# A merge's gate products issued between the steps of two attentions, with score tiles sharing PSUM banks

## What is computed

```python
h = rms_norm(x, g_norm1[l]) * (1.0 + sc1) + sh1
u = h @ w_in[l] + b_in[l]
q_lat, kv_lat, k_rope, q_sb, k_sb, v_sb, gate_mla, gate_sb = jnp.split(u, IN_SPLIT_POINTS, axis=-1)
...
y_mla = causal_softmax_attention(q, k, v_mla)           # 4 heads, 192 per head for q and k, 128 for v
y_sb = stick_breaking_attention(q_sb, k_sb, v_sb)       # 4 heads of 128
# stick breaking: l = log_sigmoid(-z) before the diagonal; a = exp(z + reverse_cumsum_keys(l)); y = a @ v
merged = (jax.nn.sigmoid(gate_mla) * (y_mla @ w_branch_mla[l])
          + jax.nn.sigmoid(gate_sb) * (y_sb @ w_branch_sb[l]))
x = x + gt1 * (merged @ w_out[l])
```

## Time and profile before

| what | value |
|---|---|
| median of 3 runs | 3700.75 us (3700.08, 3700.75, 3716.53) |
| span of the profiled execution | 3710.6 us |
| PE busy | 3287.6 us (89%) |
| DVE, ACT, POOL busy | 1128.7, 652.6, 189.4 us |
| chain that ended last | PE 83%, DMA 6%, DVE 5%, issue 4%, ACT 3% |

### The profile page before, as it was taken

The page is one execution under the profiler, slowest core; times in us unless marked ns, Lnnn a source line. Parts: engine busy times, 40 slices in busy tenths (PEclk is TensorE's granted clock), DMA queues, the critical chain, the costliest instruction groups (busy, mean ns, idle before and its releaser), DMA issues.

```text
span 3710.6 us, 31672 instructions
## 1 busy us (share of the span) xinstructions
PE 3287.6 (89%) x12207; PEld 1758.7 (47%) x12207; DVE 1128.7 (30%) x1863; ACT 652.6 (18%) x1152; POOL 189.4 (5%) x228
## 2 busy tenths in 40 slices
PE   5899974688959999969889999999899898999998
PEld 3356443544448877723444434444333443344444
DVE  3433557576731111132420023330113310133310
ACT  1221231200111111122221111110122211111100
POOL 0000001400001111020000000000000000000000
PEclk7956977898969999979969999999999899999999
DMA  5200100475639999831101122222111001322211
GB/s 202 68 0 2 44 1 1 162 279 218 250 140 346 354 353 346 293 116 57 46 0 48 48 87 69 91 68 79 58 68 45 1 0 68 113 68 68 86 67 40
DMA packets 232674, 412.87 MB, mean 111 GB/s; under 512 B 8177, under 2 KB 137757, under 8 KB 232429
## 3 DMA queue, kind: packets, MB, share of 16 engines
q1 hardware_dynamic: 204800, 314.59, 24.6%
q0 software_dynamic: 27232, 95.51, 7.1%
q10 hardware_dynamic: 525, 1.19, 0.1%
HBM read 386.08 MB, written 25.19 MB: 111 GB/s over the span
## 4 chain that ended last, share of the span: by engine, by line
PE 83%; DMA 6%; DVE 5%; issue 4%; ACT 3%; SPq 0%; POOL 0%; ACTq 0%; POOLq 0%; DVEq 0%
PE PSALL L432 49%; PE PSALL L2029 8%; PE PSALL L1473 6%; PE PSALL L1481 3%; DMA AR<-idx_rows 2%; PE PSALL L644 2%; PE PSALL L1701 1%; PE PSALL L663 1%; DMA W<-in_w_branch_b 1%; PE PSALL L403 1%; PE PSALL L1028 1%; PE PSALL L1916 1%; DMA AR<-hn_rows,AR 1%; PE PSALL L1915 1%; PE PSALL L654 1%
## 5 line engine op out<-in xcount | busy, mean ns | idle before, releaser
L432 PE MATMUL PSALL<-HN,W 128*128 128x512 f32 x2880 | 1270.7, 602 | 73.7 <-DMA W<-in_w_branch_b 30.5
L432 PEld LDWEIGHTS PSALL<-HN,W 128*128 128x128 f32 x2880 | 549.8, 192 | 783.0 <-issue 749.1
L432 PE MATMUL PSALL<-AR,W 128*128 128x512 f32 (+1 forms) x784 | 352.5, 604 | 8.6 <-DVE AR L491 5.5
L2029 PE MATMUL PSALL<-AR,W 128*128 128x512 f32 x704 | 302.5, 592 | 0.0
L1473 PE MATMUL PSALL<-AR,W 128*128 128x128 f32 x2560 | 291.4, 276 | 8.1 <-DVE AR L1514 8.1
L1473 PEld LDWEIGHTS PSALL<-AR,W 128*128 128x128 f32 x2560 | 288.2, 192 | 11.6 <-issue 11.5
L432 PEld LDWEIGHTS PSALL<-AR,W 128*128 128x128 f32 (+1 forms) x784 | 148.9, 191 | 200.3 <-issue 200.3
L2029 PEld LDWEIGHTS PSALL<-AR,W 128*128 128x128 f32 x704 | 133.8, 190 | 168.4 <-issue 168.4
L2007 DVE TENSOR_SCALAR AR<-AR,VEC 128x512 f32<-128x512 f32 x88 | 42.9, 488 | 391.0 <-ACT AR L1987 391.0
L515 DVE TENSOR_TENSOR H<-H,TMP 128x512 f32<-128x512 f32 x40 | 27.7, 691 | 414.4 <-ACT TMP L500 414.4
L432 PE MATMUL PSALL<-W,HN 128*128 128x512 f32 x320 | 146.0, 608 | 4.4 <-DVE W L986 4.4
(11 more groups left out here) (411 smaller groups left out, 2923.2 us busy)
## 6 DMA issues: line engine op xcount, KB each, us to landing
W<-in_w_up SPq DMA_DIRECT2D x84, 1024.0 KB
W<-in_w_in SPq DMA_DIRECT2D x26, 2048.0 KB
AR<-in_w_ada POOLq DMA_DIRECT2D x24, 2048.0 KB, 8.4
W<-in_w_gate SPq DMA_DIRECT2D x40, 1024.0 KB
W<-in_w_down SPq DMA_DIRECT2D x40, 1024.0 KB
y_rows<-AR SPq DMA_DIRECT2D x40, 512.0 KB, 10.7
AR<-in_ada_w POOLq DMA_DIRECT2D x8, 2048.0 KB, 8.5
W<-in_w_down SPq DMA_DIRECT2D x8, 2048.0 KB
```

Source lines behind the costliest of these rows:

```text
L432: mm = pe.matmul(o, l, r, start=(i == 0), stop=(i == len(products) - 1))
L2029: mm = pe.matmul(PS[g % 4][:, :], w[:, k - k0, m * P:(m + 1) * P], FF[:, k, :], start=(k == 0), stop=(k == FT - 1))
```

## The change

A second PE generator, `gate_steps`, makes the 16 gate groups of a layer (128 products) and is pulled by `fill(n)` between the steps of both attentions: 40 products in `sb_pe`, 88 in `mla_pe`. The gates alternate between banks 6 and 7, so a gate group waits until the gate two before it is read out. To free these banks, triangular tiles share banks: `tri(slot, j)` puts the tiles of one head into three banks (512 wide alone, 384 and 128 together, 256 alone). The readers wait until both tiles of a shared bank are written, and the order of the tiles changes. ACT copies the gates raw into 16 SBUF tiles that are free by then (`GATE`), at places written out in `sb_act` and `mla_act`; the sigmoids are made in place later by `branch_act`. The merge is replaced by `branch_pe`, with the 16 branch groups only, and `branch_dve` multiplies straight out of PSUM. The weight blocks are reordered: 17 to 20 are the gates, 21 and 22 the branches, with their ends in `LAYER_END` to match.

```diff
-        def group_steps(pe, g, it, products, tiles_ready=None):
+        def group_steps(pe, g, it, products, tiles_ready=None, bank=None, ahead=3):
             v = g if it is None else it[0] * it[1] + g
+            bank = g % 4 if bank is None else bank
             if it is not None or g >= 4:
-                pe.wait_ge(proj_taken, v - 3)
+                pe.wait_ge(proj_taken, v - ahead)
...
+        SUM_ORDER, SUMMED = (2, 3, 1, 0), {2: 1, 3: 3, 1: 3, 0: 4}
+        MAX_ORDER, SCORED, MAXED = (0, 2, 1, 3), (2, 3, 2, 4), (2, 3, 3, 4)
+        def tri(slot_, j):
+            return PS[3 * slot_ + (0, 1, 2, 1)[j]][:, (0, 0, 0, 384)[j]:(512, 384, 256, 512)[j]]
+        def gate_steps(pe, L):
+            it, gi = (L, L_BLOCKS), (L, L_GROUPS)
+            for i in range(16):
+                n, m = LB + 17 + i // 4, i % 4
+                if m == 0:
+                    arrived(pe, n, it)
+                yield from group_steps(pe, LG + GL["gate"] + i, gi, channel_products(slot(n), m, HN), bank=6 + i % 2, ahead=1)
+        def gates_act(act, L, first, steps):
+            last = steps // 8
+            for i in range(first, last):
+                act.wait_ge(proj_done, L * L_GROUPS + (LG + GL["gate"] + i + 1))
+                act.activation(GATE[i], PS[6 + i % 2][:, :], ACT.Copy).then_inc(proj_taken, 1)
+            return last
...
             scores(0)
             scores(1)
+            fill(16)
             sums(0)
             sums(1)
             weigh(0)
+            fill(2)
             scores(2)
             weigh(1)
+            fill(2)
             scores(3)
+            fill(16)
             sums(2)
             sums(3)
             weigh(2)
+            fill(4)
             weigh(3)
...
+                taken = gates_act(act, L, taken, (8, 0, 24)[pair])
+                weights(pair)
+                taken = gates_act(act, L, taken, (16, 0, 36)[pair])
+                result(pair)
+                weights(pair + 1)
+                result(pair + 1)
+            return gates_act(act, L, taken, 40)
...  (mla_pe)
             scores(0)
             for h in range(MH):
+                fill(6)
                 if h >= 1:
                     pe.wait_ge(la_out, L * 4 + h)
                 for t in range(NT):
                     pe.wait_ge(la_p, L * 16 + (4 * h + t + 1))
                     ... transposes of tile t
+                    if t < NT - 1:
+                        fill(4)
                 if h + 1 < MH:
                     scores(h + 1)
+                fill(4)
                 ... V product
...  (mla_act, with base = 40 + 22 * h)
+                    if t >= 2:
+                        taken = gates_act(act, L, taken, 40 + 22 * h + (6, 10)[t - 2])
                 ... the four copies of the transposed tiles
+                taken = gates_act(act, L, taken, 40 + 22 * h + 18)
                 ... the copy of the result
+                taken = gates_act(act, L, taken, 40 + 22 * h + 22)
...
+        def branch_pe(pe, L):
+            for c in range(KC):
+                ...
+                group(pe, LG + GL["branch"] + 2 * c, gi, channel_products(wa, m, YM, 4))
+                group(pe, LG + GL["branch"] + 2 * c + 1, gi, channel_products(wb, m, YS, 4))
+        def branch_dve(dve, L):
+            for c in range(KC):
+                dve.wait_ge(gate_open, L * KC + (c + 1))
+                for b in range(2):
+                    g, tile = LG + GL["branch"] + 2 * c + b, gate_tiles(c)[b]
+                    dve.wait_ge(proj_done, L * L_GROUPS + (g + 1))
+                    dve.tensor_tensor(tile, tile, PS[g % 4][:, :], ALU.mult).then_inc(proj_taken, 1)
+                dve.wait_ge(proj_taken, L * L_GROUPS + (LG + GL["branch"] + 2 * c + 2))
+                dve.tensor_tensor(YT[1][:, c, :], *gate_tiles(c), ALU.add).then_inc(merged, 1)
...
-        LAYER_END = {12: 3, 13: sbg(3), 14: 20, 15: sbg(7), 16: sbg(11), 17: 45, 18: 46, 19: 47, 20: 61, 21: 62, 22: 63, 23: 67, 24: 71}
+        LAYER_END = {12: 3, 13: sbg(3), 14: 20, 15: sbg(7), 16: sbg(11), 17: 35, 18: 39, 19: 43, 20: 47, 21: 55, 22: 63, 23: 67, 24: 71}
```

More of the change, by code:

```diff
@@ L428, in group_steps @@
                     n *= s
-                o = PS[g % 4][0:m, 0:n]
+                o = PS[bank][0:m, 0:n]
                 if len(r.shape) == 3:
@@ L1592, in build @@
         LG = B1_GROUPS
-        GL = {"lat": 0, "qn": 5, "qr": 9, "kn": 13, "vm": 17, "merge": 32, "out": 64, "up": 72, "down": 116}
+        GL = {"lat": 0, "qn": 5, "qr": 9, "kn": 13, "vm": 17, "gate": 32, "branch": 48, "out": 64, "up": 72, "down": 116}
         BESIDE = 6
@@ L1685, in sb_proj_act, with sb_pe, fill @@
                 act.activation(VSB[:, m, :], b[:, :], ACT.Copy).then_inc(proj_taken, 1)
-        def sb_pe(pe, L):
+        SUM_ORDER, SUMMED = (2, 3, 1, 0), {2: 1, 3: 3, 1: 3, 0: 4}
[15 more added lines that the diff above has]
+            return last
+        def sb_pe(pe, L, beside):
+            def fill(n):
+                for _ in range(n):
+                    next(beside)
             def scores(h):
@@ L1906, in heads_norm_dve, with score, mla_pe, fill @@
             rotate(2 * MH - 1)
-        def mla_pe(pe, L):
+        def score(t):
+            return tri(0, 3 - t)
+        def mla_pe(pe, L, beside):
+            def fill(n):
+                for _ in range(n):
+                    next(beside)
             def scores(h):
-                for t in range(NT):
+                if h >= 1:
+                    pe.wait_ge(la_e, L * 16 + 4 * h)
+                for t in MAX_ORDER:
                     ts_, n = slice(t * P, (t + 1) * P), (t + 1) * P
[L1913 to L1917, removed]
+                    pe.matmul(score(t), QN[:, h, ts_], KN[:, h, 0:n], start=True, stop=False)
+                    pe.matmul(score(t), QR[:, h, ts_], KR[:, h, 0:n], start=False, stop=True)
+                    pe.matmul(score(t)[:, t * P:n], ident, mask["ncaus"], start=False, stop=True, skip_group_check=True
                               ).then_inc(la_s, 1)
@@ L1952, in mla_dve @@
         def mla_dve(dve, own, L):
             for h in range(MH):
[L1954 to L1957, removed]
+                for t in MAX_ORDER:
+                    i = 4 * h + t
+                    dve.wait_ge(la_s, L * 16 + (4 * h + SCORED[t]))
+                    own(dve.tensor_reduce(NMX[:, i:i + 1], score(t), AX_X, ALU.max))
@@ L2224, in _ @@
                 heads_norm_pe(pe, L, sb_proj)
-                sb_pe(pe, L)
-                mla_pe(pe, L)
+                gates = gate_steps(pe, L)
+                sb_pe(pe, L, gates)
+                mla_pe(pe, L, gates)
+                for _ in gates:
+                    pass
                 pe.wait_ge(la_out, L * 4 + 4)
-                merge_pe(pe, LB + 17, LG + GL["merge"], it, gi, YM, YS)
+                branch_pe(pe, L)
                 out_pe(pe, L + 1, LB + 23, LG + GL["out"], it, gi, norm=L * 2 + 4)
@@ L2326, in _ @@
                 mla_dve(dve, own, L)
-                merge_dve(dve, own, L + 1, LG + GL["merge"], gi)
+                branch_dve(dve, L)
                 residual_dve(dve, own, L * 2 + 1, LG + GL["out"], gi)
```

79 lines of the change are left out of this document (48 added, 31 removed).

## The result

The changed kernel takes 3559.41 us, the median of 4 runs (3555.98 to 3563.81), beside 3706.00 us of the kernel before (4 runs). The ratio is 0.9595, with a 95% interval of 0.9573 to 0.9617. The forecast was 3576 us in a range of 3550 to 3628 us.

A forecast was written before the change was run, and what follows sets the result against it. PE bounds the merge; the attentions are bound by latency, with PE waiting or slow. Attentions and merge save 140.6 us, less debits of 6 and 5 us: -130 us, giving 3571 to 3586 us, taken as 3576 us, range 3550 to 3628 us.

The forecast's parts named there:

- 1.00 in the mixture: Softmax attention with gate products among its small ones: holes filled, clock near 1.00; the forecast's own case, chance 0.68.
- ten transposes: Each softmax attention head: ten transposes of PE, put at 1.8 to 2.9 us from profile rows, taken as 2.7 us.
- allowance for dips: Debit for clock dips and short waits in between: 2.5 us per layer, 5 us in all.
- 3 us for the slow start: Start of each layer's attentions: PE has just waited and its clock is low; debit 3 us per layer, 6 us in all.
- the two ends: Forecast time counted from the median run or the profiled execution: 3571 us and 3586 us, with 3576 us taken.
- tail of the merge: End of the merge: PE's wait for the last addition falls from 2.75 to 1.5 us, a gain of 1.3 us per layer.
- 1.5 us margin on gate 2: Stick breaking's second fill: ACT's copy is done after 8.8 us, PE has 10.3 us of products; fits by 1.5 us.
- case 3: Gates come free late, ACT having them behind exponentials and logarithms, so PE stands: 32 us more, 3608 us; chance 0.08.
- Cases 2 and 4: Softmax attention: clock falls in each head, 38 to 76 us more, chance 0.15; or stays 1.2 GHz throughout, 3821 us, 0.04.
- the 12 us at 0.50: Profile row of softmax attention before the change: 12.00 us of scores without a gap, in which PE remained at 1.2 GHz.
- The rule that the prediction set against the row: Trainium skill: activity releases the throttle and sustained work gets the full clock, so filling the gaps is enough.
- Case 5: Fills delay scores that DVE and ACT wait for, idle time returns: merge's 34 us or nothing gained, 3667 to 3700; chance 0.05.

The follow-up runs named there:

- margin: The changed kernel with four gate products moved from stick breaking's second fill of 16 to before scores 3 (2, 6, 12); 3561.80 us in one run.
- no_fill: The changed kernel with every fill taken out of both attentions, all 128 gate products of a layer together behind softmax attention; 3681.57 us, ratio 0.993.

## Why the prediction was right, point by point

The mechanism was right in every step that could be read: where the holes were, that the fills are longer than the waits, which waits have no cover, that bank sharing costs softmax attention nothing and ACT's copies hold PE up nowhere, that the DMA waits go, and that the clock follows. The last of these was the least well founded: 1.00 in the mixture rested on one window of another stage and a chance of 0.68, and nothing in the sum derived it. What was off were sizes, all to one side. By the forecast's own terms, per layer:

| term | forecast, us | measured, us |
|---|---|---|
| stick breaking with 34.3 us of gates, 0.7 wait, 3 for the start | 77.0 | 74.9, 76.4 |
| softmax attention with 75.5 us of gates, 0.9 wait, 2.5 for dips | 125.8 | 116.6, 116.6 |
| branch stage | 56.4 | 56.8, 56.8 |

In softmax attention, 9.2 us per layer too much, the mis-sized term is the **ten transposes**. I priced them at 2.7 us per head from rows in which they stood between waits; beside gate products they cost 0.11 us each, 0.11 + 0.22 + 0.33 + 0.43 = 1.09 us per head, by the starts in the timeline above. That is 6.4 us per layer. The allowance for dips, 2.5 us, was not needed: 1.00 throughout. The V product is 2.16 us and not 2.26 (0.4 us here; with the scores of stick breaking, also 2.16, 0.8 us there), because the 2.26 was read right behind a wait; and the last wait is 0.7 instead of 0.9. The scores, 1906.09 to 1912.86, are the 6.77 us of the forecast. The 3 us for the slow start were right for the second layer (16 score instructions took 7.36 us, at full clock 4.3) and too much for the first. In all 20 us, the 150.0 us measured in the stages against 130 forecast. The base was uncertain by as much: later runs put the kernel before at 3706 to 3714 us, not at the 3700.75 of the three shown. 3576 us amounts to a base of 3706 us, the median measured beside the changed kernel; no row told where between the two ends it lay, so that this was met is luck. The 17 us by which the forecast is off are thus all in the saving (20 us in the traces). Nor is 3716.5 us the time of the profiled execution: in the other runs the time is 1.6 to 3.0 us above the profiled span, which makes it 3712 to 3714, and the upper end 3582 to 3584 us. The measured time lies below both ends, by the transposes and the dips most of all.

The tail of the merge became 1.58 us, forecast 1.5. The 1.5 us margin on gate 2 is in the trace too: ACT's copy of it ran to 1858.75 us, 8.9 us behind scores 3 (8.8 summed), and PE wanted the bank at about 1860.2.

Of the rivals, case 3 (gates free late) is real only where margin put it. Cases 2 and 4 rested on the 12 us at 0.50. The row was true and my reading of it was incomplete: it showed what scores with 64-row products among them do behind a fallen clock, not that gapless work can't regain it. The rule that the prediction set against the row held for the mixture: with 75.5 us of 128-row products in 116 us it ran at 1.00, even where they came in one lump per head. Case 5 fell at once: behind the fills PE found DVE and ACT always ahead.

## What to carry to other kernels

Where one stage is bound by latency and its neighbour by TensorE, look for products that need nothing of the first, and issue them between its steps: count each hole, count the products, and check that no buffer that they need is freed by an engine that is itself late in the same hole. Read the clock beside busy time: of the 81 us that the fills in softmax attention saved in the traces, 11 us per layer were waits (81.17 - 70.00 in no_fill) and the other 29 us nearly all clock. Before that, issue the 128-row products of a stage first and the shallow ones together behind them, or pad the shallow operand with zeros; it was worth 1.0 to 1.4% of the kernel before here by itself and needs no new schedule.

## What the hardware did that I had not expected

A 64-row product among 128-row ones costs TensorE 0.39 us for its two changes of depth, at full clock (0.96, 1.05 and 0.32 us against 0.86, 0.86 and 0.22), and a stage that alternates eight times per head stayed at 0.50 for 12 us without a gap. The same products with the 128-row ones first, or the same product filled up with zeros, let the clock come back within a head's scores: 72 to 82 us became 57 to 58.5 us. Whether the changes or the 64 rows keep the clock low stays open.
